# One list of loads by due time, weight and chunk rings of 6 and 5, operands made ahead of the conversions, and latent products normalised behind the matmuls

## The reference

```python
mod = silu(c) @ w_ada + b_ada                  # shift, scale, gate for mixer and MLP
h = rms_norm(x, norm_mix) * (1 + sc_a) + sh_a
p = h @ w_in                                   # 2048 x 3912, cut into cq 512, ckv 256, kr 64, sb, fox, f
q  = rms_norm(p_cq, q_norm) @ w_uq             # latent attention: 512 -> 8 x (128 + 64)
kv = rms_norm(p_ckv, kv_norm) @ w_ukv          # 256 -> 8 x (128 + 128)
# rope on q's and k's last 64; block-causal softmax attention (MLA), 8 heads
# stick-breaking attention on p_sb, forgetting attention on p_fox, 8 heads of 64 each
o = concat of the three, rms-normed per head
x = x + g_a * (o @ w_out)
h = rms_norm(x, norm_ffn) * (1 + sc_m) + sh_m
x = x + g_m * (relu(h @ w_ff1) ** 2 @ w_ff2)
out = rms_norm(x, final_norm)
```

## Time and profile before

| | us |
|---|---|
| median of 3 runs | 1244.07 |
| lowest, highest | 1241.99, 1255.64 |
| profiled execution: time, span | 1249.44, 1247.6 |
| mean granted TensorE clock in it | 0.958 |
| TensorE busy, VectorE, ScalarE, GpSimd | 1135.6, 749.2, 518.9, 292.5 |
| moved from and to memory | 296.87 MB, mean 238 GB/s |

### The profile page before, as it was taken

How to read it: one execution, slowest core, us unless ns; L and a number is a source line. 1 busy time by engine, 2 the same in 40 slices (tenths; PEclk the granted TensorE clock), 3 DMA queues, 4 the chain that set the end, 5 groups by cost and what they waited for, 6 DMA issues and landing times.

```text
span 1247.6 us, 21662 instructions
## 1 busy us (share of the span) xinstructions
PE 1135.6 (91%) x9084; PEld 1091.3 (87%) x9084; DVE 749.2 (60%) x963; ACT 518.9 (42%) x627; POOL 292.5 (23%) x143
## 2 busy tenths in 40 slices
PE   6868787768979989799999999999999999999996
PEld 5757687758857889699999999999999999999995
DVE  4578373736578666697787745444455555455454
ACT  3523323233635434354444433333344444444341
POOL 3845657543731559400000000000000000000000
PEclk8989898979889989989999999999999999999998
DMA  9977676737986459947878666566656656555651
GB/s 369 355 296 308 258 289 242 299 123 268 363 311 204 129 203 396 370 169 280 302 274 308 221 204 197 191 195 194 194 180 207 198 188 200 190 197 173 215 191 68
DMA packets 81311, 296.87 MB, mean 238 GB/s; under 512 B 9024, under 2 KB 9152, under 8 KB 81216
## 3 DMA queue, kind: packets, MB, share of 16 engines
q1 hardware_dynamic: 81216, 295.50, 67.3%
HBM read 293.37 MB, written 2.10 MB: 237 GB/s over the span
## 4 chain that ended last, share of the span: by engine, by line
PE 67%; DMA 11%; POOL 7%; DVE 6%; issue 4%; ACT 4%; SPq 1%; DVEq 0%; ACTq 0%; POOLq 0%
PE ps L1224 40%; PE ps L1230 20%; DMA raw<-in_weights 10%; POOL w_lo L715 5%; PE ps L1395 2%; ACT w_hi L435 2%; DMA ada<-in_ada 2%; DVE ada L810 2%; PE ps L1242 1%; DVE o_tok L1127 1%; ACT tmp L467 1%; SPq L381 1%; PE ps L1247 0%; PE ps L1405 0%; PE ps L1266 0%
## 5 line engine op out<-in xcount | busy, mean ns | idle before, releaser
L435 ACT ACTIVATE w_hi<-raw 128x1024 fp32r<-128x1024 f32 x362 | 381.2, 1059 | 571.0 <-PE ps L1230 360.0
L791 DVE TENSOR_TENSOR w_lo<-raw,w_hi 128x1024 fp32r<-128x1024 f32 x256 | 315.2, 1240 | 265.6 <-ACT w_hi L435 264.9
L1224 PE MATMUL ps<-hT,w_hi 128*128 128x256 f32 x3072 | 394.9, 282 | 55.3 <-DVEq L878 31.6
L1224 PEld LDWEIGHTS ps<-hT,w_hi 128*128 128x128 f32 x3072 | 375.8, 193 | 61.4 <-DVEq L878 34.7
L715 POOL TENSOR_TENSOR w_lo<-raw,w_hi 128x1024 fp32r<-128x1024 f32 x106 | 253.9, 2413 | 169.6 <-ACT w_hi L435 169.3
L1224 PE MATMUL ps<-act,w_hi 128*128 128x256 f32 x2048 | 252.9, 276 | 0.0
L1224 PEld LDWEIGHTS ps<-act,w_hi 128*128 128x128 f32 x2048 | 241.6, 188 | 0.0
L1230 PE MATMUL ps<-hT,w_lo 128*128 128x256 f32 x1536 | 209.6, 279 | 3.5 <-POOL w_lo L715 3.4
L1230 PEld LDWEIGHTS ps<-hT,w_lo 128*128 128x128 f32 x1536 | 191.9, 190 | 5.3 <-POOL w_lo L715 5.3
L709 POOL TENSOR_TENSOR ssq<-ssq,sq 128x1024 f32<-128x1024 f32 x6 | 14.4, 2408 | 657.6 <-ACT sq L442 657.6
L1230 PE MATMUL ps<-act,w_lo 128*128 128x256 f32 x1024 | 136.9, 276 | 0.0
(11 more groups left out here) (202 smaller groups left out, 832.0 us busy)
## 6 DMA issues: line engine op xcount, KB each, us to landing
raw<-in_weights SPq DMA_DIRECT2D x362, 512.0 KB, 4.3
ada<-in_ada SPq DMA_DIRECT2D x165, 512.0 KB, 6.0
ada_more<-in_ada SPq DMA_DIRECT2D x27, 512.0 KB, 6.9
xT<-in_xt SPq DMA_DIRECT2D x4, 512.0 KB, 7.4
y<-tmp SPq DMA_DIRECT2D x2, 512.0 KB, 2.6
consts<-in_consts SPq DMA_DIRECT2D x1, 580.0 KB, 4.7
y<-sq SPq DMA_DIRECT2D x1, 512.0 KB, 2.6
y<-ssq SPq DMA_DIRECT2D x1, 512.0 KB, 2.6
```

The costliest lines, as they stand in the source:

```text
L435: sc.activation(w_hi[:, slot, :, :], raw[:, slot, :, :], ACT.Copy).then_inc(hi_done, 1)
L791: ve.tensor_tensor(w_lo[:, slot, :, :], raw[:, slot, :, :], w_hi[:, slot, :, :].bitcast(F32), ALU.subtract).then_inc(lo_vec, 1)
L1224: pe.matmul(acc[:, n, :], w, rhs[:, kt0 + k, half, :], start=first and k == 0 and n % 2 == 0 and half == 0, stop=False, skip_group_check=True)
```

## The change

Four things change up to the output projection; the feed-forward half stays.

1. **One list of loads** (`load_order`). Each unit and chunk gets a due time in units of TensorE's progress, and SP issues them sorted by it. The unit ring `raw` has 6 slots up to unit 47 and 4 from 48 on (`RAWS`, `U_WIDE`); the two more lie in `more`. The chunk ring has 5 slots up to chunk 59, then 4. `w_hi` and `w_lo` keep 4.
2. **Mix operands earlier.** ScalarE makes a part's operand at the start of a block, one block earlier than before, and not behind that block's conversions. VectorE makes the low part behind the block's chunks. Three of the four normed tiles of x (`xn`) move from VectorE to GpSimd.
3. **Latents unnormalised.** The operand is the latent times its gain; ScalarE makes its high part, GpSimd the low part (`lat_lo`). The root is taken beside it, its Newton steps run at the end of the projection (`invert_latents`), and VectorE multiplies it onto the products when it reads them from PSUM; for the values, which lie turned, ScalarE does so with one number per partition (`read_values`), for which TensorE sums the squares once more with tokens on the partitions.
4. **Chunk tables.** 80 and not 82 chunks lie in the projection, 23 and not 28 in the 8 latent steps, 25 and not 20 in the softmax steps, 32 and not 30 in the output projection. In step 6 VectorE copies the first outputs ahead of its chunks.

```diff
-A_EARLY = 18
+A_EARLY = 16
-WIDE = 7
+SHIFT = 1
+WIDE, RAWS = 5, 6
+U_WIDE = 48
...
+def raw_slot(u):
+    return u % RAWS if u < U_WIDE else u % RING
+def raw_before(u):
+    return u - RAWS if u < U_WIDE + RING else u - RING
...
+        def load_order():
+            units = list(range(U_IN))
+            units += [U_IN + 2 * t for t in range(7) for _ in LAT_OF[t]]
+            units += [T_OUT + j for j in range(U_OUT + AHEAD)]
+            due = [(units[max(0, u - RING)] + SHIFT, 0, u) for u in range(B_FF + AHEAD)]
+            for p, n in enumerate(PARTS):
+                for b in range(BLOCKS):
+                    due += [(8 * PART_AT[p] + n * b, 1, a) for a in ada_in_part(p, b)]
...
+            return [(kind, n) for _, kind, n in sorted(due)]
...
             def load_unit(u):
-                if u >= RING:
-                    sp.wait_ge(*lo_ready(u - RING))
+                if u >= RAWS:
+                    sp.wait_ge(*lo_ready(raw_before(u)))
...
+            for kind, n in load_order():
+                if kind:
+                    load_ada(n)
+                else:
...
+                    load_unit(n)
...
             for p, n in enumerate(PARTS):
                 for b in range(BLOCKS):
+                    if p + 1 < len(PARTS):
+                        if b == (7 if p else 6):
+                            mix_operand(PART_AT[p + 2] - 1)
+                        if b == 4 and PARTS[p + 1] == 2:
+                            mix_operand(PART_AT[p + 1])
                     for _ in range(n):
                         hi(0, 0, 0, u)
                         u += 1
...
-                    elif p + 1 < len(PARTS):
-                        if b == 4:
-                            mix_operand(PART_AT[p + 1])
-                        if b == (6 if n == 1 else 7):
-                            mix_operand(PART_AT[p + 2] - 1)
-                    elif b == 3:
+                    elif b == 2:
                         sc.wait_ge(part_done, 8 * p + 2)
                         sc.activation(sq[:, :, :], pT[:, T_CQ:T_CQ + 4, :], ACT.Square).then_inc(sq_done, 1)
...
+                        lat_operand(0)
...
             for u in range(U_IN + 4):
                 lo(u)
+                if u in (U_IN - 5, U_IN - 3, U_IN - 1):
+                    lat_lo((u + 5 - U_IN) // 2)
+                if u in (3, 11, 15):
+                    b = (3, 11, 15).index(u) + 1
+                    gp.tensor_tensor(xn[:, 4 * b:4 * b + 4, :], xT[:, 4 * b:4 * b + 4, :],
...
                     if last and b == 4:
                         latent_means()
-                        invert(2, halves=2)
-                        for m in range(2):
-                            scaled_pair(R_CQ + m, pT[:, T_CQ + 2 * m:T_CQ + 2 * m + 2, :],
...
+            invert_latents()
...
+            def read_latent(n):
+                ve.wait_ge(unit_used, B_LAT + LAT_OF[n][-1] + 1)
...
+                if n < 3:
+                    ve.scalar_tensor_tensor(out=dests[n], in0=quarters(latents), scalar=(NOPE + ROPE) ** -0.5, in1=r,
+                                            op0=ALU.mult, op1=ALU.mult).then_inc(latent_read, 1)
+                else:
+                    ve.tensor_tensor(dests[n], quarters(latents), r, ALU.mult).then_inc(latent_read, 1)
```

More of the change, by code:

```diff
@@ L227, in hybrid_block @@
         y0 = el[:, :, 0:S]
+        y_lat = pt[:, :, 0:S]
+        kv_r, kv_y, kv_t = small[:, 0:2], small[:, 2:4], small[:, 4:6]
         fx, fl = tmp2[0:H, 3, :], tmp2[0:H, 2, :]
@@ L338, in ada_room, with raw_room @@
             slot = ada_slot(a)
-            return ada[:, slot, :] if slot < ADA else ada_more[:, slot - ADA, :]
+            return ada[:, slot, :] if slot < ADA else more[:, slot - ADA, :]
+        def raw_room(u):
+            slot = raw_slot(u)
+            return raw[:, slot, :, :] if slot < RING else \
+                more[:, WIDE - ADA + slot - RING, :].rearrange("p (k n) -> p k n", k=UK)
+        def load_order():
[6 more added lines that the diff above has]
+                    due += [(8 * PART_AT[p] + n * b, 1, a) for a in ada_in_part(p, b)]
+            for t in range(STEPS):
+                due += [(U_IN + 2 * t if t < H else U_IN + 2 * H + 1.2 * (t - H), 1, a) for a in ada_at(t)]
+            for j in range(U_OUT):
+                due += [(T_OUT + 2 + j, 1, a) for a in ada_out(j)]
+            due += [(T_OUT + 2 + U_OUT + 2 * m, 1, A_GM + m) for m in range(ADA)]
+            return [(kind, n) for _, kind, n in sorted(due)]
         def scaled(n):
-            return n - 16 if n >= R_FFN else n - 8
+            return n - R_FFN
         def z_bank(i):
@@ L536, in _, with read_values @@
                         sc.activation(qk[:, 8:12, :], qk[:, 8:12, :], ACT.Copy, scale=DH ** -0.5).then_inc(q_scaled, 1)
-            dests = [q_nope[:, 0:4, :], q_nope[:, 4:8, :], rope_raw[:, :, :], k_nope[:, 0:4, :],
-                     k_nope[:, 4:8, :], v_mla[:, :, 0:BW], v_mla[:, :, BW:2 * BW]]
-            def read_latent(n):
-                sc.wait_ge(unit_used, B_LAT + LAT_OF[n][-1] + 1)
-                src = latents if n >= 5 else quarters(latents)
-                sc.activation(dests[n], src, ACT.Copy, scale=(NOPE + ROPE) ** -0.5 if n < 3 else 1.0)\
-                    .then_inc(latent_read, 1)
+            def read_values(n):
+                sc.wait_ge(unit_used, B_LAT + LAT_OF[5 + n][-1] + 1)
+                for t in range(2):
+                    ins = sc.activation(v_mla[:, t, n * BW:(n + 1) * BW], latents[:, t, :], ACT.Copy,
+                                        scale=kv_r[:, t:t + 1])
+                ins.then_inc(latent_read, 1)
             def soft_parts(i):
@@ L949, in _ @@
             ve.sem_inc(psum_free, 1)
-            ve.wait_ge(c_spread, 2)
-            for a in range(2, 8):
+            for a in range(3, 8):
                 ada_tile(a)
@@ L968, in _ @@
                             mix_gain(PART_AT[p + 1])
-                        if p and b == (7 if n == 1 else 6):
+                        if p and b == 6:
                             mix_gain(PART_AT[p + 2] - 1)
@@ L972, in _ @@
                         ada_tile(a)
-                    if not last:
-                        if p == 0 and b == 6:
-                            mix_lo(1)
-                        if p and b == 4:
-                            mix_lo(PART_AT[p + 1])
-                        if p and b == 7:
-                            mix_lo(PART_AT[p + 2] - 1)
                     if p == 2 and b >= 6:
@@ L1076, in _ @@
                 todo = list(ada_at(t))
-                for a in todo[:1]:
-                    ada_tile(a)
+                if t == 6:
+                    read_group(0)
+                if t == H:
+                    ve.wait_ge(psum_ready, READY_ROT)
+                    ve.tensor_tensor(tmp2[:, :, :], quarters(latents), sin4, ALU.mult).then_inc(rope_turned, 1)
+                if t == 0:
+                    read_latent(0)
                 if t < H:
                     softplus(t)
-                for a in todo[1:]:
+                ahead = 2 if len(LAT_OF[min(t, 6)]) > 1 else 1
+                for a in todo[:ahead]:
+                    ada_tile(a)
+                if 1 <= t < 5:
+                    read_latent(t)
+                for a in todo[ahead:]:
                     ada_tile(a)
@@ L1087, in _ @@
                                           ALU.mult, ALU.add).then_inc(forget_step, 1)
[L1088 to L1090 removed]
                 if 0 <= t - H < SOFT:
                     soft_max(t - H)
[L1093 to L1094 removed]
+                if t == 10:
+                    read_group(1)
                 if t == H + 4:
```

187 lines of the change are left out of this document (100 added, 87 removed).

## The result

The changed kernel takes **1173.52 and 1175.22 us** in two of its four executions (median of all four 1186.34), the kernel before on the same chip 1241.99 to 1255.64; the ratio is **0.9416, with an interval of 0.9283 to 0.9548**. The profiled execution took 1175.22 us (span 1173.4), 74.2 less than the profiled one of before; the forecast sum had 50 less.

A forecast was written before the change was run, and what follows sets the result against it. Bound: chained waits in the input projection, no engine full. Projection -43, attention -11, softmax +1, output projection +3 sum to -50 us from 1249.44; less 5.4 for the median, 1194 us. Range 1173 to 1224.

The forecast's parts named there:

- What bounds the kernel: Input projection: a stage of waits, where VectorE waits for ScalarE, ScalarE for a load, the load for VectorE.
- The sum for the projection: Input projection: 58.0 us removed, +6 for part 1, +9 for late loads, net -43 us, ending near 248.
- +9 for loads "newly late": Input projection: with DMA at 87% and in-order issue some units will be late, +9 us, between 0 and 27.
- +6 for part 1: Input projection, part 1: VectorE can't go below about 30 us, so only some 5 of 11.2 us come.
- What was removed: Input projection: 44.8 us of TensorE's waits and 13.2 us of slow starts go, 58.0 us together.
- The x-norm tiles to GpSimd: Input projection: three VectorE operations become three on GpSimd, covered by its idle time; 7.7 us without cover.
- The list's ring of 6: Load list: the weight ring of 6 gives a load two units more, 5.4 us.
- The attention steps: Attention steps: waits and slow starts of 17.2 us go, +6 us is given back, net -11 us.
- The softmax steps: Softmax steps: VectorE gets 25 chunks and not 20 and fits barely, +1 us, between 0 and 6.
- A: Whole kernel: loads become the bound, saved time returns as ScalarE's waits for weights, 1220 us; chance 0.20.
- D: Long projection parts: slower, chunk ring of 5 makes SP stand longer with weight units behind, 1266 us; chance 0.06.
- B: Projection and attention: all of it gained, nothing comes back, -69 us, 1175 us; chance 0.08.

The follow-up runs named there:

- e1: Kernel before with only the load list, rings of 6 and 5, and ScalarE's first conversion behind its first operand: 1216.7 to 1218.5 us, ratio 0.9802.
- e2: Kernel before with only the mix operands earlier, low parts behind the chunks, and one chunk-table row: 1215.3 to 1219.7 us, ratio 0.9799.
- e3: Kernel before with load list and earlier operands together; latents, x-norm tiles and chunk tables as before: 1183.9 to 1192.7 us, ratio 0.9573.
- e5: Changed kernel with the low parts of operands 1 to 7 all made by GpSimd: 1164.21 to 1168.0 us, ratio 0.9364.
- e4: Changed kernel with only the low part of operand 1 moved to GpSimd, behind unit 9: 1164.15 to 1173.5 us, ratio 0.9388.
- e10: Changed kernel with the three later x-norm operations back on VectorE: 1161.87, 1161.93 and 1164.07 us, ratio 0.9308.
- e11: e5 with a weight ring of 4 and not 6: 1166.0 to 1168.96 us, ratio 0.935.
- e6: Changed kernel with a weight ring of 4 instead of 6, list and chunk ring of 5 kept: 1165.82 to 1170.38 us, ratio 0.9391.
- e9: Changed kernel with the chunk tables of before from the attention steps on: 1178.83 us in a single execution, no ratio.
- e8: Changed kernel with the old load order, weight ring of 4 and chunk ring of 7: 1203.97 to 1211.23 us, ratio 0.9704.
- e7: Changed kernel with one x-norm operation of GpSimd behind unit 12, not 11: 1170.57 to 1172.28 us, ratio 0.9377.
- e0: Changed kernel run once more, unaltered: 1176.41 us in a single execution.

## Why the prediction was right, and where it was not

The sign held, and the range just so: its low end is 1173, and the two times are 1173.52 and 1175.22. The forecast of 1194 was 20 us too high, and the place inside the range is partly luck, since two errors cancel in the projection (below). That waits of TensorE would go without new ones for loads was right. Step by step:

**What bounds the kernel.** Right that the stage is one of waits, and right on each wait. That they close a circle is not borne out: each half of the change takes 25 us, and together they take what they take alone (e1, e2, e3).

**The sum for the projection** was wrong in size: -43 against -58.7, and -68.0 in e5 (261.7 to 193.7). Its signs show the same: the stage ends at 229.4 and not near 248, the long parts take 43.7 us and not 47 to 53. What failed are a deduction and a term that was left out. The +9 for loads "newly late" was 0: TensorE waits 1.7 us for conversions in the whole stage. The DMA share of 0.93 is even above the 0.85 that I gave, and part 3 runs at 0.99 and 389 GB/s without a gap. I had argued from one queue with in-order issue; but a list in due order makes what stands behind a waiting chunk, as a rule, what is needed later. The +6 for part 1, put on VectorE's work, was nearly right: without the lock part 1 takes 31.9 us in e4 and 28.1 in e5, where I gave 30 as the least; VectorE has 27.2 us of work in it in e4. What I did not have is the lock. It adds a wait of 8.24 us at the end of part 0, which takes 33.5 us and not the 29.2 of before, and its slow unit and the second wait lie in part 1, 34.5 us. Parts 0 and 1 together take 68.0 us after 65.3; with operand 1 on GpSimd (e4) part 2 begins 8.8 us sooner.

**What was removed** was undersized too. I added up the waits that I could name, 44.8 us, and 2.2 us for each of six slow starts, 13.2. The stage has a floor that gives the whole at once: 64 units at 2.72 us are 174.1. By the earlier trace rows the five parts have 202.6 us busy of 261.7: 59.1 idle, and 28.5 busy above the floor, of which the small products of part 4 are some 4 (47.61 us for its 16 units now), so 24 are running at low clock, not 13. After the change, 16.1 us are idle and 12.8 above the floor. So idle time fell by 43.0 and busy time by 15.7, which is 58.7; the 58.0 that I took as removed came in full by the wrong road, with 10 or so of the lock set against 10 that I had not named.

**The x-norm tiles to GpSimd** stood in the sum at nothing, as covered by GpSimd's idle time. Wrong in kind: GpSimd has the time, but VectorE then lacks the pauses in GpSimd's row. I had the rule on the lock at hand, worked it out as 4 us for three other operations, and left it out of the sum; its price, at the place where GpSimd has no pause, is 8.2 us of waiting and a slow start, with some 2 us and another slow start in part 1, and e10 is 12 us faster.

**The list's ring of 6**, "two units more, 5.4 us": worth 0 to 4 us (e11 against e5), and in the changed kernel, where it takes GpSimd's pauses away, nothing that the times show (e6).

**The attention steps**: -14.4 for -11. The wait for the copy (5.7) is 0. Of the waits for the reads, 4.9 before, and of the +6 given back, 2.5 us are there in all (1.3 and 1.2 us on `tmp` and `q_nope`). The tables have 5 of it in the one execution of e9. The rest is not separated by a run.

**The softmax steps** 0.0 for +1 (VectorE has 49.5 of 52.5 us, as worked out), **the output projection** +1.5 for +3; by e9 0.9 of it is the two chunks. **The start** 3.1 us sooner was not in the prediction. The edit has ScalarE's first conversion no longer ahead of the root and the operand, which is the likely reason; no run has it alone.

**The rivals.** A (loads the bound) is refuted: ScalarE waits 52.0 us for loads. D is refuted: SP stands less in front of chunks, and they are not what is due. B, "nothing comes back", to which I gave 0.08, had the right size, 1175, for a partly wrong reason: no load came back as a wait, but 10 us of the lock did. One statement about the kernel before needs mending: the room of the three chunk slots is taken later by the latent operands (`lat`), not by the attention scratch.

## What to carry to other kernels

Read a stage of waits against its floor, units times what one takes with nothing in its way, before adding up named waits; idle time and slow running together are what can come back. When an operation is moved to GpSimd, ask not only whether GpSimd has time but whether it still has pauses where VectorE must get through with two SBUF inputs. Order loads of several kinds by one due time before spending room on deeper rings. And read two runs that differ by one edit for what else differs: here e8 and the changed kernel differed by the long wait too.

## What the runs showed of the hardware

- A VectorE subtraction with both inputs in SBUF was held up over a row of GpSimd operations on SBUF: 9.43 (changed kernel), 9.35 (e9), 9.83 (e4), 7.10 (e7) and 4.38 us (e0) where it takes 0.69. In all but e0 it ended some 0.5 us after GpSimd's row.
- In e8 the granted clock fell from 2.4 to 1.2 GHz behind gaps of 0.33, 0.58 and 1.21 us that lie within 8 us of small products (TensorE was busy 9.67 of the 10 us up to 300), and stayed down for some 45 us in which TensorE was busy all the time. In the projection it was back some 6 us after a long wait: in the changed kernel it is 0.50 of full speed from 60 to 64 us, behind the wait of 8.24, and 1.00 from 66, with weight units all the while.
- Loads went at 389 GB/s over 43.68 us of part 3, with TensorE never waiting for one. The Trainium skill ("DMA: Bandwidth & Descriptors", Where 436 GB/s comes from) has about 358 GB/s as the limit of memory per core, half of what a stack gives two cores, and lets it bind between memory and SBUF; this kernel, on one core, went above it over a whole part, and the measurement decides.
